# Recurrent mixer of a two-block kernel: gate projections of all steps first, exponentials two steps ahead, value products one step later

## The reference

```python
wl = w0 + einsum('btzr,zrc->btzc', tanh(lw), w_lora_b)          # low-rank gate, two directions
decay = exp(-exp(-softplus(-wl) - 0.5))                         # = exp(-C0 * sigmoid(wl))
a = sigmoid(a0 + einsum('btzr,zrc->btzc', la, a_lora_b))        # low-rank gate
kk = heads(k * k_k); kk = kk * rsqrt(max(sum(kk * kk), 1e-12))
k_dir = k * (1.0 + (a - 1.0) * k_a)
def step(s, inp):                                               # scan over tokens, per direction
    s_kk = einsum('bhvk,bhk->bhv', s, kk_t)
    s = s * w_t - s_kk[..., None] * (kk_t * a_t) + v_t[..., None] * k_t
    return s, einsum('bhvk,bhk->bhv', s, r_t)
```

## Time and profile before

| | us |
|---|---|
| median of three runs | 1931.67 (1928.92 to 1936.48) |
| profiled execution | 1917.69 |
| its span | 1915.9 |
| PE busy | 1742.4 (91%) |
| DVE busy | 1081.8 (56%) |
| ACT busy | 757.2 (40%) |
| POOL busy | 197.6 (10%) |
| mean granted clock of PE | 0.94 of full speed |

### The profile page before, as it was taken

One profiled execution on the slowest core, in us unless ns is written; L12 is line 12 of the kernel. 1 busy time (PEld: TensorE's weight loads), 2 busy tenths in 40 slices (PEclk: granted clock), 3 DMA queues, 4 the chain that ended last, 5 costly groups with the idle time before them and its releaser, 6 DMA issues.

```text
span 1915.9 us, 26646 instructions
## 1 busy us (share of the span) xinstructions
PE 1742.4 (91%) x11391; PEld 1500.2 (78%) x11391; DVE 1081.8 (56%) x1263; ACT 757.2 (40%) x835; POOL 197.6 (10%) x233
## 2 busy tenths in 40 slices
PE   5599989778568889999999999999999999999997
PEld 1378876556458689899999999877899977799996
DVE  5736646456566754665555555666644565654555
ACT  1224314443143343333343333455534455544344
POOL 0002260341232000070000000000000000000000
PEclk8699999786679889999999999999999999999999
DMA  7548540000333534455455555542454544335551
GB/s 284 177 164 283 203 78 1 6 20 4 80 87 139 206 130 176 163 185 180 176 176 188 189 193 178 176 166 105 146 191 176 186 166 176 110 143 177 198 196 67
DMA packets 150239, 289.66 MB, mean 151 GB/s; under 512 B 32431, under 2 KB 35582, under 8 KB 150121
## 3 DMA queue, kind: packets, MB, share of 16 engines
q1 hardware_dynamic: 135224, 270.47, 40.3%
q0 software_dynamic: 4960, 13.94, 2.5%
q10 hardware_dynamic: 9936, 3.54, 0.7%
HBM read 281.56 MB, written 6.37 MB: 150 GB/s over the span
## 4 chain that ended last, share of the span: by engine, by line
PE 79%; DVE 10%; ACT 3%; issue 3%; DVEq 2%; DMA 2%; ACTq 1%; POOLq 0%; SPq 0%; POOL 0%
PE psum L201 22%; PE psum L203 21%; PE psum L202 21%; DVE w_low L171 2%; PE psum L1365 1%; PE psum L1337 1%; PE psum L272 1%; DVE blk L1069 1%; PE psum L271 1%; PE psum L266 1%; ACT w_high L166 1%; DVE outer L1066 1%; PE psum L684 1%; DVE AtE L1059 1%; DVE w_low L189 1%
## 5 line engine op out<-in xcount | busy, mean ns | idle before, releaser
L171 DVE TENSOR_TENSOR w_low<-raw,w_high 128x4096 fp32r<-128x4096 f32 x105 | 464.9, 4428 | 314.6 <-ACT w_high L166 312.3
L166 ACT ACTIVATE w_high<-raw 128x4096 fp32r<-128x4096 f32 x107 | 386.6, 3615 | 274.7 <-DMA raw<-in_moe_w_dram 141.0
L201 PE MATMUL psum<-act_high,w_high 128*128 128x256 f32 (+1 forms) x1176 | 337.3, 287 | 5.8 <-DVE w_low L171 5.8
L202 PE MATMUL psum<-act_low,w_high 128*128 128x256 f32 (+1 forms) x1176 | 336.3, 286 | 0.0
L203 PE MATMUL psum<-act_high,w_low 128*128 128x256 f32 (+1 forms) x1176 | 336.3, 286 | 0.0
L201 PEld LDWEIGHTS psum<-act_high,w_high 128*128 128x128 f32 x1176 | 227.7, 194 | 11.4 <-issue 10.1
L202 PEld LDWEIGHTS psum<-act_low,w_high 128*128 128x128 f32 x1176 | 227.6, 194 | 1.2
L203 PEld LDWEIGHTS psum<-act_high,w_low 128*128 128x128 f32 x1176 | 227.5, 193 | 0.7
L203 PE MATMUL psum<-actA_high,w_low 128*128 128x256 f32 x512 | 144.9, 283 | 0.0
L202 PE MATMUL psum<-actA_low,w_high 128*128 128x256 f32 x512 | 144.9, 283 | 0.0
L201 PE MATMUL psum<-actA_high,w_high 128*128 128x256 f32 x512 | 144.8, 283 | 0.0
(11 more groups left out here) (490 smaller groups left out, 3131.3 us busy)
## 6 DMA issues: line engine op xcount, KB each, us to landing
raw<-in_moe_w_dram SPq DMA_DIRECT2D x48, 2048.0 KB, 8.3
raw<-in_w_in_dram SPq DMA_DIRECT2D x20, 2048.0 KB, 8.1
raw<-in_w_up_dram SPq DMA_DIRECT2D x16, 2048.0 KB, 8.8
raw<-in_w_down_dram SPq DMA_DIRECT2D x16, 2048.0 KB, 7.7
modw<-in_mod_w_dram SPq DMA_DIRECT2D x12, 2048.0 KB, 11.2
raw<-in_w_out_dram SPq DMA_DIRECT2D x6, 2048.0 KB, 8.4
raw<-in_w_gate_dram SPq DMA_DIRECT2D x4, 2048.0 KB, 8.5
gates_d<-gstage ACTq DMA_DIRECT2D x8, 256.0 KB, 6.4
```

Source lines behind the costliest of these rows:

```text
L166: act.activation(WH[n % NSLOT][:, 0:elems], RAW[n % NSLOT][:, 0:elems], ACT.Copy).then_inc(s_wh, 1)
L171: dve.tensor_tensor(WL[n % NSLOT][:, 0:elems], RAW[n % NSLOT][:, 0:elems], WH[n % NSLOT][:, 0:elems].bitcast(F32), ALU.subtract).then_inc( ...
L201: pe.matmul(o, aH, wH, start=start, stop=False)
L202: pe.matmul(o, aH, wL, start=False, stop=False)
```

## The change

The diff below is cut to the parts that set the order; wait conditions were renumbered throughout. In words:
- The gate products of all eight steps come first, two steps' banks in turn, with their adds and their activations, into eight buffers each for ew and ea. Sigmoid is replaced by tanh of half the argument, with the factors moved into scales and biases (tok_c, tok_b) of the exponentials, into kab, and into the factor -0.5 of B and of Mq. POOL computes kkn for all four chunks ahead.
- In step p the engines then prepare step p + 2: cumulation, sums and exponentials. Ktk, Rtk and Kb exist twice.
- Transposes and state products take turns in banks 0 and 1, all grams in banks 4 and 5; the value products of a step that came last in it follow in the step after.
- A units, and B units of steps 0 to 3, are copied by ACT without a mask (`gram_scalar`). The triangle of blk is selected by POOL once it is back (`blocks_pool`).
- The table `quota` is gone, and the 30 pivots of b = 0 stand behind the last mask and the last sum into yacc.
- PE begins only when the attention's result yb is out of its banks.

```diff
-    ew = s1.take("ew", [P, DA])
-    ea = [s1.take(f"ea{i}", [P, DA]) for i in range(2)]
-    kkn = s1.take("kkn", [P, DA])
...
+    kkn_off = s1.at
...
+    kkn = [sb(f"kkn{i}", [P, DA], F32, kkn_off + 2 * KB * i) for i in range(4)]
...
+        return 4 + g % 2
+
+    def gram_out(q, g):
+        q.wait_ge(R["gA" if G_ENGINE[g] == "act" else "ge"], G_COUNT[g])
+
+    TURNS = [("col", 0), ("col", 1)]
     for p in range(NP):
-        for i, (kind, u) in enumerate(units(p)):
-            b = unit_bank(kind, u)
-            before[p, kind, u] = last.get(b)
-            last[b] = gu0(p) + i
-        for b in range(2):
-            before[p, "end", b] = last[b]
-            before[p, "end", 4 + b] = last[4 + b]
+        TURNS += [("B", p), ("K", p)] + ([("R", p)] if p >= 4 else []) + [("V", p)]
+        if keeps(p) or p + 2 < NP:
...
         pool.drain().then_inc(s_const, 1)
 
     def rwkv_pool(pool):
+        pool.wait_ge(R["kr"], 2 * NT + 2)
+        pool.wait_ge(s_uev, NW)
+        for i in range(4):
+            tt = PS[2 * i][1]
+            pool.tensor_tensor(kkn[i][:, :], z_k[:, tt, :], kkb[:, :], ALU.mult)
+            pool.drain()
+            pool.tensor_tensor(hv(kkn[i][:, :]), hv(kkn[i][:, :]), bc(krs[:, H * tt:H * tt + H], HD), ALU.mult)
+            pool.drain().then_inc(R["pooled"], 1)
         for p in range(NP):
             prep_on_pool(pool, p)
-        pool.wait_ge(R["tr"], tr0(NP))
-        pool.wait_ge(R["d0"], d00(NP))
+            if p == 5:
+                blocks_pool(pool, 0)
+        blocks_pool(pool, 1)
+        pool.wait_ge(R["tr"], len(TURNS))
         for q in range(4):
             pool.memset(Tt0[q][:, :, :], 0.0)
             pool.memset(Tm[q][:, :, :], 0.0)
...
+    def blocks_pool(pool, b):
+
+        pool.wait_ge(R["blk"], 16 * (b + 1))
+        pool.affine_select(out=blk[:, :, :], in_=blk[:, :, :], compare_op=ALU.is_ge, fill=0.0, base=-1,
+                           pattern=[[-1, 32], [1, 32]], channel_multiplier=0)
+        pool.drain().then_inc(R["tri"], 1)
+
+
+    def lora_vector(dve, p):
+
+        d = PS[p][0]
+        b = 6 if p % 2 == 0 else 4
+        dve.wait_ge(R["lora"], p + 1)
+        dve.tensor_tensor(ew[p][:, :], psum[:, b, :], w0b[:, d, :], ALU.add)
+        dve.tensor_tensor(ea[p][:, :], psum[:, b + 1, :], a0b[:, d, :], ALU.add)
+        dve.drain().then_inc(R["loraE"], 1)
...
+    def prep_vector(dve, p):
+
+        tt = PS[p][1]
+        dve.wait_ge(R["cum"], p + 1)
+        if p >= 2:
+            dve.wait_ge(R["tr"], T_AT["K", p - 2] + 1)
+        dve.tensor_tensor(Ktk[p % 2][:, :], psum[:, cum_bank(p), :], ew[p][:, :], ALU.subtract
+                          ).then_inc(R["vprep"], 1)
+        if p >= 1:
+            dve.wait_ge(R["pooled"], ks_at(p - 1))
+        dve.scalar_tensor_tensor(out=kdir[:, :], in0=ea[p][:, :], scalar=-1.0, in1=kab[:, :],
+                                 op0=ALU.add, op1=ALU.mult)
+        dve.drain()
+        dve.wait_ge(R["pooled"], KQ + p // 2 + 1)
+        dve.scalar_tensor_tensor(out=ea[p][:, :], in0=ea[p][:, :], scalar=1.0, in1=kkn[p // 2][:, :],
+                                 op0=ALU.add, op1=ALU.mult)
+        dve.scalar_tensor_tensor(out=kdir[:, :], in0=kdir[:, :], scalar=1.0, in1=z_k[:, tt, :],
+                                 op0=ALU.add, op1=ALU.mult)
+        dve.drain().then_inc(R["vprep"], 1)
+
+    def key_vector(dve, p):
+
+        dve.wait_ge(R["exps"], p + 1)
+        dve.tensor_tensor(Ktk[p % 2][:, :], Ktk[p % 2][:, :], kkn[p // 2][:, :], ALU.mult)
+        dve.drain().then_inc(R["vprep"], 1)
...
-            dve.wait_ge(R["blk"], 16 * (b + 1))
+            dve.wait_ge(R["tri"], b + 1)
...
     def rwkv_vector(dve):
-        quota = {4: [0] * 4 + [2] * 4, 5: [1] * 10, 6: [1] * 8, 7: [1] * 4 + [0] * 6}
...
+            lora_vector(dve, p)
+            if p in (2, 3):
+                prep_vector(dve, p - 2)
+            if p in (3, 4):
+                key_vector(dve, p - 3)
+        for p in range(NP):
+            if p + 2 < NP:
+                prep_vector(dve, p + 2)
+            if p > 0:
+                y0_vector(dve, p - 1)
+            for kind, u in units(p):
+                if kind == "C" or (kind == "B" and p >= 4):
+                    mask_vector(dve, p, kind, u)
+            if p + 2 < NP:
+                key_vector(dve, p + 2)
+        y0_vector(dve, NP - 1)
+        for k in range(30, 0, -1):
+            pivot_vector(dve, 0, k)
+        inverse_vector(dve, 0)
...
+    def tanh_scalar(act, p):
+        act.wait_ge(R["loraE"], p + 1)
+        act.activation(ew[p][:, :], ew[p][:, :], ACT.Tanh, scale=0.5)
+        act.activation(ea[p][:, :], ea[p][:, :], ACT.Tanh, scale=0.5)
+        act.drain().then_inc(R["tanh"], 1)
+
+    def exps_scalar(act, p):
+        d = PS[p][0]
+        act.wait_ge(R["vprep"], 3 * p + 1)
+        k = Ktk[p % 2]
+        act.activation(k[:, :], k[:, :], ACT.Exp, bias=tok_c[:, d, 2:3], scale=-0.5 * C0)
+        if p >= 1:
+            act.wait_ge(R["pooled"], ks_at(p - 1))
+        act.activation(epos[:, :], psum[:, cum_bank(p), :], ACT.Exp, bias=tok_c[:, d, 0:1], scale=0.5 * C0)
+        if n_of(p) == 2:
+            act.wait_ge(R["tr"], T_AT.get(("R", p - 2), 0) + 1)
+            act.activation(Rtk[p % 2][:, :], psum[:, cum_bank(p), :], ACT.Exp, bias=tok_c[:, d, 1:2],
+                           scale=-0.5 * C0)
+        act.drain().then_inc(R["exps"], 1)
...
+    def gram_scalar(act, p, kind, u):
+
+        i0, _ = unit_heads(p, kind, u)
+        g = G_AT[p, kind, u]
+        act.wait_ge(R["gu"], g + 1)
+        if kind == "A" and u == 0 and p > 1:
+            act.wait_ge(R["dia1"], 64 * (p // 2))
+        dst = Apf if kind == "A" else AtE0[p]
+        act.activation(dst[:, i0:i0 + 4, :], bank3(gram_bank(g)), ACT.Copy).then_inc(R["gA"], 1)
+
+    def x0_scalar(act, p):
+        act.wait_ge(R["xu"], cu0(p + 1))
+        i = act.activation(X0(p)[:, :], psum[:, 2, :], ACT.Copy)
+        if p >= 4 and PS[p][0] == 0:
+            i = act.activation(yacc[:, PS[p][1], :], psum[:, 3, :], ACT.Copy)
+        i.then_inc(R["x0E"], 1)
...
-        prep_scalar(act, 0, 2)
         for p in range(NP):
...
+            tanh_scalar(act, p)
+            if p in (2, 3):
+                turn_out(act, "col", p - 2)
+                exps_scalar(act, p - 2)
+        for p in range(NP):
             if p > 0:
-                act.wait_ge(R["gu"], gu0(p))
...
+                act.wait_ge(R["gu"], G_AT[p, "B", 0])
+            for kind in ("B", "K", "R", "V"):
+                if (kind, p) in T_AT:
+                    turn_out(act, kind, p)
+            if p + 2 < NP:
+                exps_scalar(act, p + 2)
+            if ("state", p) in T_AT:
+                turn_out(act, "state", p)
+            if p > 0:
+                x0_scalar(act, p - 1)
+            for kind, u in units(p):
+                if kind == "A" or (kind == "B" and p < 4):
+                    gram_scalar(act, p, kind, u)
+        x0_scalar(act, NP - 1)
         blocks_out(act, 1, 3)
         blocks_in(act, 1)
         blocks_back(act, 0, True)
...
+    def turn_tensor0(pe, kind, p):
+
+        i = T_AT[kind, p]
+        b = i % 2
+        if i >= 2:
+            pe.wait_ge(R["ev"], i - 1)
...
-        prep_tensor(pe, 0, 1)
-        pe.wait_ge(s_const, 2)
-        prep_tensor(pe, 0, 2)
+        pe.wait_ge(s_yb, NT)
         for p in range(NP):
-            d, tt = PS[p]
-            if p + 1 < NP:
-                prep_tensor(pe, p + 1, 1)
-            transposes_tensor(pe, p)
-            if p + 1 < NP:
-                prep_tensor(pe, p + 1, 2)
-            if keeps(p):
-                if p > 0:
-                    pe.wait_ge(R["ge"], before[p - 1, "end", 5] + 1)
-                state_tensor(pe, p, Kb, z_v[:, tt, :], 5).then_inc(R["d0"], 1)
-                pe.wait_ge(R["ev"], ev_tr(p) + 1)
-            pe.wait_ge(R["ev"], ev_tr(p))
+            lora_tensor(pe, p)
+            if p in (2, 3):
+                pe.wait_ge(s_const, 2)
+                cum_tensor(pe, p - 2)
+                turn_tensor0(pe, "col", p - 2)
+        for p in range(NP):
+            pe.wait_ge(R["pooled"], ks_at(p))
+            pe.wait_ge(R["vprep"], 3 * p + 3)
+            for kind in ("B", "K", "R", "V"):
+                if (kind, p) in T_AT:
+                    turn_tensor0(pe, kind, p)
+            if p + 2 < NP:
+                cum_tensor(pe, p + 2)
+            if ("state", p) in T_AT:
+                turn_tensor0(pe, "state", p)
+            if p > 0:
+                for u in ((0, 1) if p - 1 < 4 else (2, 3)):
+                    value_tensor(pe, p - 1, u)
+            pe.wait_ge(R["ev"], last_turn(p) + 1)
             gram_tensor(pe, p, "B", (0, 1))
-            gram_tensor(pe, p, "C", (0, 1))
             if p >= 4:
                 gram_tensor(pe, p, "B", (2, 3))
+            gram_tensor(pe, p, "C", (0, 1))
+            if PS[p][0] == 1:
+                gram_tensor(pe, p, "A", (0, 1))
+            if p >= 4:
```

(6 more changed lines are left out.)

363 lines of the change are left out of this document (159 added, 204 removed).

## The result

| | before | after |
|---|---|---|
| median of four runs, us | 1930.30 | 1956.67 |
| profiled execution | 1917.69 | 1957.36 |
| its span | 1915.9 | 1955.6 |
| mean granted clock of PE | 0.94 | 0.925 |

The changed kernel is slower: ratio 1.0141, 95% interval 1.0092 to 1.0190. The forecast was 1952.7 with a range of 1936 to 1970, so direction and size are right. Not all parts of the sum are: on the traces they add to 18 us more than foreseen.

The account below looks back on a forecast made before the run. It took PE's work at a mixed clock plus waits for masks or copies as the bound, then a chain of waits after the last step; +18 - 15 - 19 + 35 + 2 = +21 on 1931.67 gave 1952.7 us, range 1936 to 1970.

Parts of the forecast that it names:

- parts of the sum: Five terms in us: mixer preparation +18, steps 0 to 3 -15, steps 4 to 7 -19, hand-over +35, attention ahead +2.

Follow-up runs that it names:

- pivots_between: The changed kernel with the 30 pivots of the first half and their inverse back between the masks of steps 4 to 7; 1922.7 us, ratio 0.9978 to before.

## What to carry to other kernels

When work moves, cost what it was hidden under: 30 pivots that were free between masks cost 31 us at a place where everything waits for them, and eight memsets behind them in an idle engine's queue cost 10 more. A new wait on PE can have two prices, the wait and the clock behind it, and the second was here between as much as the first and four times it; look for each wait that a change adds, even one of 1.5 us. Filling PE's gaps paid where the steps hung on PE (11 us), and not in the old order, where PE still waited for DVE behind the fillers: the clock rose and the time stayed. And do not credit an edit with a clock that one trace shows: the same code ran at 0.93 and at 0.74.

## What the runs showed of the hardware

- An idle time of 1.54 us on PE, behind the small matmuls that end the attention, was followed by a preparation at a mean clock of 0.56, 0.63, 0.66 and 0.79 in four traces; without it the same matmuls ran at 0.85 and 0.89. In the changed kernel PE was listed as busy for 26.1 of those 28.9 us and stayed at half clock for most of them; in pivots_between it was back at full clock within 5 us.
- Unread matmuls, most of them 384 wide, in PE's gaps of 1.3 to 1.5 us in steps 4 to 7 went with a clock of 0.97 to 0.98 and 73.0 to 73.4 us in three traces, against 0.67 to 0.83 and 82.2 to 92.8 us in eight without. For steps 0 to 3 no such thing is shown: with four gate pairs more and no fillers they ran at 0.93 and at 0.74.
- A DVE product of two SBUF inputs took 0.68 alone and 2.17 when it began while POOL ran a selection on SBUF with 1.63 us to go: it waits for nearly all that is left.
- The same program, in the same stage, ran 11 us longer at a clock of 0.93 instead of 0.99 to 1.00 in two stretches of 150 us. Two profiles of a kernel are the least that is needed before a difference of half a per cent is given a place.
